# Streaming encoder step on one core: first tile's v-row sums moved into the u stage, the dots' x rows moved to SBUF, and the first tile's dots put ahead of later routing

## The chip, the core and the metric

The kernel runs on one core of one Trainium2 chip. The metric is the time of one execution on the device in microseconds (us), and lower is better. TensorE is PE in the rows, VectorE is DVE, ScalarE is ACT, GpSimd is POOL, SyncE is SP.

## What is computed

One layer for 1024 prompt tokens and 32 sample tokens of width 1024: sparse and forgetting attention, an output projection, cross-attention into 256 memory tokens, and a mixer that picks, for each token, 16 of 16384 single-neuron experts in each of 8 heads. The change is in the mixer:

```python
def blk(xb):                                  # 128 tokens
    q = (xb @ w_q).reshape(TOK_BLOCK, PEER_HEADS, PEER_KEY_DIM)
    s1 = jnp.einsum('thd,hnd->thn', q[..., :half], keys1)
    s2 = jnp.einsum('thd,hnd->thn', q[..., half:], keys2)
    v1, i1 = lax.top_k(s1, PEER_TOPK)
    v2, i2 = lax.top_k(s2, PEER_TOPK)
    ...
    g = jax.nn.softmax(sv, axis=-1)           # sv, eidx: the best 16 of the 16 x 16 sums
    h = jax.nn.gelu(jnp.einsum('td,thkd->thk', xb, u[eidx]), approximate=False)
    return jnp.einsum('thk,thkd->td', (g * h).astype(v.dtype), v[eidx])
```

## The kernel before

The 1056 tokens are split in two kinds. Four tiles of 128 tokens and the 32 sample tokens (544 tokens, columns 0 to NSP) are **sparse**: their chosen rows of u and v are gathered from HBM. Each gather is one indirect DMA that GpSimd issues; it takes its 128 row numbers from one column of an index tile in SBUF and brings 128 rows of 4 KB (0.52 MB), one per partition. One gather serves one token, whose 8 x 16 experts lie on the 128 partitions. The other 512 tokens are **dense**: they are multiplied with all experts.

The program is a row of blocks that follow each other on all engines. Those of interest:

- **Mixer stage** (dense tokens' projections, `route`, first part): 40 weight blocks of 128x1024 (8 w_out, 8 w_mq, then attention, 8 w_mo, 16 w_pq). Each is rounded by ScalarE, its remainder is taken by GpSimd ("split", L1041), and TensorE makes 24 matmuls of it (L1062).
- **u stage** (`route`, second part): 128 blocks of u. For each, ScalarE rounds (L1591), GpSimd splits (L1596, both inputs in SBUF), TensorE makes 24 matmuls (L1606), ScalarE applies Gelu (L1614), SyncE stores 256 KB and loads the block four further on (512 KB). There are two buffers: block n+2 is rounded when product n is done.
- **Gates stage** (`spread_gates`): one-hot matmuls for the dense tokens' gates, and 24 batches of v sums.
- **v stage** (`experts`): 128 blocks of v for the dense tokens (L2884, split on GpSimd at L2968), and between them the remaining v sums.

**Routing and dots.** VectorE does the top-k work in nine slots (`slot(j)`: tiles 0 to 3, the sample tokens, tiles 4 to 7), in 21 steps each. The list of routing instructions is a generator; `progress.fill(us)` in the mixer stage takes pieces up to a budget, and the u stage takes all the rest. Between the steps stand the **dots**: for token d, `dot(d)` (L1943) multiplies the gathered u row with the token's x row and sums to one column of `hn`. The x row of the current tile lies in PSUM (`row_flat`, 2 banks), spread over the partitions and put there by ScalarE in `show_rows`, which waits until the dots of the tile before are done. `DOTS_AT[j]` says how many dots go into slot j, `CHUNKS_AT[j]` how many u blocks TensorE does beside it.

**GpSimd's queue.** It holds split n+2 and then the gathers due beside block n, in that order, block after block. A gather waits until the dot that last used its row buffer is done (14 buffers in the u stage, 6 in the mixer stage). So gathers and splits share one queue in program order.

**v sums.** A batch is four tokens: four gathers of v rows, then 8 matmuls with the weights placed by ScalarE in a zero-padded tile (`SparseSum`, L2576). There are 136 batches, 24 in the gates stage (`B_STEPS`) and 112 in the v stage; TensorE takes them in its own queue between the products.

Of the kernel before, what the change touches and what calls it, by code (L numbers as in the profile page):

```python
# [14 lines left out]
P = 128  # L15
# [1522 lines left out]
PIECES = 40  # L1538
# [341 lines left out]
def route(nc, sem, dram, keep, mx, sems):  # L1880


    with ExitStack() as ctx:
# [6 lines left out]
        RINGS = (list(range(RING + 2)), list(range(RING + 10)))  # L1890
# [63 lines left out]
        def tail(j):  # L1954
# [33 lines left out]

        def slot(j):
# [4 lines left out]
            def ordered(op, cost):  # L1994
# [4 lines left out]
                yield cost  # L1999
                if j >= 1:  # L2000
                    yield from dots(DOTS_TO[j] + DOTS_AT[j] * min(done[0], 16) // 16)
# [184 lines left out]
        def beside_pieces(engine, u):  # L2186
# [7 lines left out]
            if u == len(LATE_UNITS) - 1:  # L2194
                reach(2, 0)

        late_attention(nc, sem, late_ctx, dram, keep, beside_load, beside_scores, beside_copy, beside_pieces)
        late_ctx.close()

        open_mixer(nc, ctx, keep, "n_", ND)  # L2200
        row_flat = keep["row_flat"]
# [3 lines left out]
                for part, a, n in (("ring", 0, RING), ("oS_flat", 2 * D, 2), ("oD_flat", 0, 4), ("q_flat", 0, 4))  # L2205
                for i in range(n)]
        hidden = DenseHidden(mx, keep, dram, mx.xh)
# [3 lines left out]
        ps, x_ps = keep["aps"][:, 0:2, :], keep["aps"][:, 2, 0:3 * P].rearrange("p (i m) -> p i m", i=3)  # L2211
        norm_q, norm_f = mx.norm(), mx.norm()
# [3 lines left out]
        def _(engine):  # L2216
# [11 lines left out]
            for n in range(MIX, QRY):  # L2228
                progress.fill(us)
                if n == QRY - 1:  # L2230
                    reach(2, TAIL)
# [6 lines left out]
            for n in range(QRY, ATT):  # L2238
                progress.fill(us)
                if n == QRY + 1:  # L2240
                    reach(2, TAIL + 1)
# [11 lines left out]
            for n in range(PKQ, END):  # L2253
                progress.fill(us + 1.0)
                if n == PKQ:
                    reach(3, S_DONE)
                if n == PKQ + 4:
                    reach(3, TAIL + 1)
# [7 lines left out]
        def _(sp):  # L2266
            load_pq(sp, 3)
            sp.wait_ge(mx.x_split, 28)
            sp.dma_start(mx.h, dram["xP"][:, :, mx.c0:mx.c0 + mx.w]).then_inc(h_loaded, 16)
            for n in range(2, 27):  # L2270
                mx.load(sp, n)
                if n == 15:
                    load_pq(sp, 4)
# [11 lines left out]
            for j in range(5, QT + 2):  # L2285
                if j < QT:
                    if j == 5:
# [3 lines left out]
                for n in chunks(j):  # L2291
                    hidden.store(sp, n)
                    if n + 4 < NKEY:
                        hidden.load(sp, n + 4)
            hidden.finish(sp)

        @block.tensor
        def _(pe):
# [30 lines left out]
            for n in range(QRY, ATT):  # L2329
# [4 lines left out]
                if n in (QRY + 1, QRY + 2):  # L2334
                    scores(3, n - QRY - 1)
                if n == QRY + 6:
                    turn(1)
# [7 lines left out]
            for n in range(PKQ, END):  # L2345
                mx.product(pe, n)
                if n in (PKQ + 3, PKQ + 4):
                    scores(4, n - PKQ - 3)
                if n == PKQ + 8:
                    turn(2)  # L2350
            for j in range(5, QT + 2):
# [14 lines left out]
        def _(act):  # L2366
# [11 lines left out]
            def show_rows(i):  # L2378

                if i > 0:  # L2380
                    act.wait_ge(x_loaded, 16 * i)
                    act.wait_ge(dotted, i * P)
                act.activation(row_flat, xrow[:, :], ACT.Copy).then_inc(row_shown, 1)
                if i < NS:
                    act.wait_ge(row_shown, i + 1)
                    act.dma_start(xrow[:, :], dram["s_x"][i]).then_inc(x_loaded, 16)

# [11 lines left out]
            show_rows(0)  # L2399
# [10 lines left out]
            for n in range(QRY, ATT):  # L2410
                next_high(n + 2)
                if n in (QRY + 2, QRY + 3):
                    copy_scores(3, n - QRY - 2)
                if n == QRY + 4:
                    exponents(act, 2)
                if n == QRY + 6:
                    keep_routes(act, 1)
# [837 lines left out]
```

## Time and profile before

| | us |
|---|---|
| median of 3 runs (3956.85 to 3971.69) | 3968.24 |
| profiled execution, its own time | 3969.84 |
| its span, first to last instruction | 3968.0 |
| mixer stage | 1357 to 1695 |
| u stage | 1695 to 2617 |
| gates stage | 2624 to 2850 |
| v stage | 2876 to 3940 |

The span of the profiled execution and its time differ by 1.8 us. PE is busy 88% of the span, DVE 62%, POOL 49%, ACT 29%. These are averages over stages with different limits, so they are to be read stage by stage: the digits of the page show POOL near idle in the first half and at 7 to 8 tenths in the u stage, where the DMA engines are at 9.

### The profile page before, as it was taken

The numbers are of one execution on the slowest core, as the hardware profiler recorded it, in microseconds if no ns is written. First come the engines' busy times: TensorE is split into PE (matmuls) and PEld (weight loads), VectorE is DVE, ScalarE is ACT, GpSimd is POOL, SyncE is SP. The second block draws the span as 40 slices with busy tenths as digits, with TensorE's granted clock in tenths as the row PEclk, the third lists the DMA queues.
The fourth block names the chain that finished last, engine by engine and source line by source line (L and its number), as shares of the span: only waits on it lengthen the run. The fifth ranks groups of instructions, "written<-read, shape, count | busy, mean of one in ns | idle before, by whom it ended". The sixth has DMA issues, their size and how long they took to land. (4 is left out here: it accounts for less than half of the span.)

```text
span 3968.0 us, 49765 instructions
## 1 busy us (share of the span) xinstructions
PE 3478.3 (88%) x17237; PEld 2501.8 (63%) x17237; DVE 2448.6 (62%) x5652; ACT 1158.6 (29%) x2264; POOL 1944.2 (49%) x1478
## 2 busy tenths in 40 slices
PE   7889887998989898887877878898689999999998
PEld 4445555788978676765666666665455556656655
DVE  3764423655857677779879697897633444434344
ACT  1213323121156523222222222266622212222222
POOL 0000001224400144778888888854267777877773
PEclk9888987998999999999999999999899999999999
DMA  2002103312431235799999999979998998989995
GB/s 117 10 33 61 55 27 123 101 54 87 140 96 33 85 121 191 278 348 377 399 396 401 400 396 401 374 253 400 329 366 324 363 360 336 392 339 351 358 374 217
DMA packets 335403, 978.48 MB, mean 247 GB/s; under 512 B 34400, under 2 KB 84456, under 8 KB 333648
## 3 DMA queue, kind: packets, MB, share of 16 engines
q0 software_dynamic: 156672, 570.49, 36.7%
q1 hardware_dynamic: 173584, 389.78, 27.9%
q10 hardware_dynamic: 4928, 15.34, 1.1%
q8 instruction: 130, 2.13, 0.2%
q14 instruction: 89, 0.73, 0.0%
HBM read 873.61 MB, written 101.89 MB: 246 GB/s over the span
## 5 line engine op out<-in xcount | busy, mean ns | idle before, releaser
L1606 PE MATMUL n_ps<-n_xh_flat,n_wh 128*128 128x512 f32 x3072 | 748.3, 401 | 162.8 <-POOL n_wh L1596 160.9
L2884 PE MATMUL e_y_ps<-e_wh,e_vh 128*128 128x512 f32 x3072 | 751.3, 401 | 45.4 <-DVE e_wh L3008 34.7
L1606 PEld LDWEIGHTS n_ps<-n_xh_flat,n_wh 128*128 128x128 f32 x3072 | 581.3, 192 | 325.2 <-POOL n_wh L1596 202.9
L2884 PEld LDWEIGHTS e_y_ps<-e_wh,e_vh 128*128 128x128 f32 x3072 | 572.1, 189 | 266.6 <-issue 130.4
L1025 POOL CAST m_wh<-raw 128x1024 fp32r<-128x1024 f32 x40 | 42.2, 1054 | 911.4 <-issue 659.0
L2968 POOL TENSOR_TENSOR e_vh<-raw,e_vh 128x1024 fp32r<-128x1024 f32 x128 | 309.2, 2418 | 225.9 <-ACT e_vh L2910 223.0
L3047 DVE TENSOR_TENSOR oT<-e_y_ps,oT 128x512 f32<-128x512 f32 x256 | 175.8, 691 | 376.0 <-PE e_y_ps L2884 303.6
L2543 POOL DMA_INDIRECT e_rows<-in_v,eid x346 | 349.1, 1009 | 99.0 <-issue 86.9
L1596 POOL TENSOR_TENSOR n_wh<-raw,n_wh 128x1024 fp32r<-128x1024 f32 x128 | 307.4, 2402 | 39.6 <-ACT n_wh L1591 37.3
L1943 DVE CUSTOM_DVE_ANT_0 oT<-oT,n_row_ps 128x1024 f32<-128x1024 f32 x227 | 270.9, 1217 | 67.9 <-DMA oT<-in_u,eid 64.4
L1062 PE MATMUL m_ps<-m_xh_flat,m_wh 128*128 128x272 f32 x1920 | 261.8, 298 | 40.7 <-DVE oT L1095 12.3
L1041 POOL TENSOR_TENSOR n_wh<-raw,n_wh 128x1024 fp32r<-128x1024 f32 x40 | 100.2, 2507 | 384.7 <-ACT n_wh L1035 384.3
L1062 PEld LDWEIGHTS m_ps<-m_xh_flat,m_wh 128*128 128x128 f32 x1920 | 254.7, 196 | 46.0 <-issue 20.6
L1062 PE MATMUL n_ps<-n_xh_flat,n_wh 128*128 128x512 f32 x960 | 240.7, 409 | 36.2 <-POOL n_wh L1041 14.9
L2576 PE MATMUL z_ps<-e_rows,flat 128*32 128x512 f32 x1384 | 255.2, 602 | 19.4 <-DMA e_rows<-in_v,eid 17.0
L1943 DVE CUSTOM_DVE_ANT_0 m_ring<-m_ring,n_row_ps 128x1024 f32<-128x1024 f32 x184 | 220.3, 1217 | 74.4 <-DMA m_ring<-in_u,eid 71.3
L1614 ACT ACTIVATE flat<-n_ps 128x512 f32<-128x512 f32 x128 | 76.5, 597 | 640.1 <-PE n_ps L1606 599.6
L2466 POOL DMA_INDIRECT oT<-in_u,eid x227 | 219.0, 965 | 62.2 <-issue 46.8
L1062 PEld LDWEIGHTS n_ps<-n_xh_flat,n_wh 128*128 128x128 f32 x960 | 185.2, 195 | 88.6 <-POOL n_wh L1041 28.2
L2910 ACT ACTIVATE e_vh<-raw 128x1024 fp32r<-128x1024 f32 x128 | 134.5, 1052 | 322.6 <-PE e_y_ps L2884 187.6
L2466 POOL DMA_INDIRECT m_ring<-in_u,eid x184 | 179.6, 976 | 69.8 <-issue 37.9
L1943 DVE CUSTOM_DVE_ANT_0 n_q_flat<-n_q_flat,n_row_ps 128x1024 f32<-128x1024 f32 x133 | 159.1, 1217 | 25.5 <-DMA n_q_flat<-in_u,eid 21.6
(390 smaller groups left out, 5698.1 us busy)
## 6 DMA issues: line engine op xcount, KB each, us to landing
raw<-in_ut SPq DMA_DIRECT2D x128, 512.0 KB
raw<-in_v SPq DMA_DIRECT2D x126, 512.0 KB
s_hid<-flat SPq DMA_DIRECT2D x128, 256.0 KB
xrow<-s_hid SPq DMA_DIRECT2D x126, 256.0 KB
s_gate<-g_stage SPq DMA_DIRECT2D x3, 8192.0 KB, 53.1
raw<-in_w_pq SPq DMA_DIRECT2D x32, 512.0 KB
m_ring<-s_gate SPq DMA_DIRECT2D x32, 512.0 KB
gh<-s_gate SPq DMA_DIRECT2D x32, 512.0 KB
```

The source lines that it names most:

```text
L1041: pool.tensor_tensor(wh[:, at % 2, LO, :], w[:, at % 2, :], wh[:, at % 2, HI, :].bitcast(F32), ALU.subtract).then_inc(self.w_split, 1)
L1062: mm = pe.matmul(self.bank(n, g), wh[:, at % 2, hw, k * P:(k + 1) * P], self.xh[:, hx, k, a:a + c], start=(k == 0 and o == 0), stop=(k == ...
L1596: pool.tensor_tensor(self.uh[:, at % 2, LO, :], self.u[:, at % 2], self.uh[:, at % 2, HI, :].bitcast(F32), ALU.subtract).then_inc(self.mx. ...
L1606: mm = pe.matmul(self.ps[:, n % 2, 0:ND], self.uh[:, at % 2, a, k * P:(k + 1) * P], self.xd[:, b, k, :], start=(k == 0 and o == 0), stop=( ...
L1943: dve.tensor_tensor_reduce(out=rows[b], in0=rows[b], in1=row_flat, scale=1.0, scalar=0.0, op0=ALU.mult, op1=ALU.add, accum_out=hn[:, d:d + ...
L2466: pool.indirect_dma_start(out=rows[b], out_offset=None, in_=dram["u"], in_offset=bass.IndirectOffsetOnAxis(ap=eid[:, d:d + 1], axis=0)).th ...
L2543: pool.indirect_dma_start(out=buffer, out_offset=None, in_=self.rows_dram, in_offset=bass.IndirectOffsetOnAxis(ap=self.idt[:, col:col + 1] ...
L2576: mm = pe.matmul(self.ps[g * 32:(g + 1) * 32, t % 2, half, :], self.wz[:, b // 4 % 2, b % 4 * P + g * 32:b % 4 * P + (g + 1) * 32], buffer ...
L2884: mm = pe.matmul(y_ps[:, o, 0:TD], vh[:, n % SLOT, a, m * P:(m + 1) * P], wh[n % SLOT][:, b, g * TD:(g + 1) * TD], start=(c == 0 and e == ...
L2910: act.activation(vh[:, n % SLOT, HI, :], v[:, n % 2, :], ACT.Copy).then_inc(v_rounded, 1)
L2968: pool.tensor_tensor(vh[:, n % SLOT, LO, :], v[:, n % 2, :], vh[:, n % SLOT, HI, :].bitcast(F32), ALU.subtract).then_inc(v_split, 1)
L3047: dve.tensor_tensor(y[:, m, cols], y_ps[:, o % 4, 0:TD], y[:, m, cols], ALU.add).then_inc(y_added, 1)
```

## The change

1. The **32 batches of the first tile** (v sums of tokens 0 to 127) are summed in the u stage, between blocks 22 and 122, in two PSUM banks of their own (`y_ps`), with their gathers in GpSimd's queue. The result goes to HBM (`s_ysp`) and is loaded again in the v stage, where it is turned and added as before. The gates stage still sums 24 batches (those of tile 1), the v stage 80 instead of 112.
2. The **x rows** of the dots lie in SBUF (`xrow` and a new `x_row`, loaded by DMA from `s_x`), no more in PSUM; `show_rows` falls away. The dot's three tensors are then all in SBUF.
3. The **128 dots of tile 0** stand in the last steps of routing slot 2, ahead of the routing of slots 3 to 8. Slots 3 and 4 keep their order, but slot 4's u blocks are now beside slot 3's routing (`FIRST_IN_U` 4), and the blocks per slot are redistributed. The row buffers are 10 instead of 14 in the u stage (the other four hold v rows and weights).
4. ScalarE's Gelu and the weighting of tile 0 come at block 12, the turn at block 18. GpSimd begins with 14 semaphore clears.

```diff
-CHUNKS_AT = (0, 0, 0, 0, 0, 18, 32, 32, 30, 12, 4)
+FIRST_IN_U = 4
+CHUNKS_AT = (0, 0, 0, 0, 27, 22, 22, 22, 21, 10, 4)
-DOTS_AT = (0, 0, 0, 64, 64, 128, 128, 128, 32, 0)
+DOTS_AT = (0, 0, 128, 64, 64, 64, 64, 80, 80, 0)
+WEIGH_AT, GELU_BLOCK, TURN_BLOCK, SUM_FROM, SUM_TO = (3, 8), 12, 18, 22, 122
+SUM_BLOCKS = tuple(SUM_FROM + b * (SUM_TO - SUM_FROM) // 31 for b in range(32))
...
-            dve.wait_ge(row_shown, d // P + 1)
+            i = d // P
+            if i > 0:
+                dve.wait_ge(x_loaded[i % 2], 16 * ((i + 1) // 2))
             b = ring.take(now[0])
             dve.wait_ge(row_ready[b], 16 * ring.uses(d))
-            dve.tensor_tensor_reduce(out=rows[b], in0=rows[b], in1=row_flat,
+            dve.tensor_tensor_reduce(out=rows[b], in0=rows[b], in1=x_rows[i % 2],
...
+        sums.ps = ctx.enter_context(nc.psum_tensor("y_ps", [P, 1, 2, 512], F32))
-        row_flat = keep["row_flat"]
+        x_rows = [xrow[:, :], sb("x_row", [P, D])[:, :]]
...
@@ tensor, u stage
                     hidden.product(pe, n)
+                    if n == TURN_BLOCK:
+                        pe.wait_ge(weighed, 1)
+                        pe.matmul(w_ps, hn[:, 0:P], ident, start=True, stop=True).then_inc(weights_turned, 1)
+                    for b in range(32):
+                        if SUM_BLOCKS[b] == n:
+                            at = [(4 * b + g) % N_ROW for g in range(4)]
+                            sums.sum(pe, b, [v_rows[i] for i in at], [v_row_ready[i] for i in at],
+                                     [16 * ((4 * b + g) // N_ROW + 1) for g in range(4)])
@@ gpsimd, u stage
-                    last = min(DOTS_TO[j] + 10, N_DOT)
+                    last = max(first, min(DOTS_TO[j] + 7, N_DOT))
                     gathers(first + -(-(last - first) * (i + 1) // CHUNKS_AT[j]))
+                    while batch < 32 and GELU_BLOCK < n and SUM_BLOCKS[batch] <= n + 6:
+                        for g in range(4):
+                            i_row = 4 * batch + g
+                            if i_row >= N_ROW:
+                                pool.wait_ge(sums.summed, (i_row - N_ROW) // 4 + 1)
+                            sums.gather(pool, batch, g, v_rows[i_row % N_ROW], v_row_ready[i_row % N_ROW])
+                        batch += 1
@@ v stage
+B_FIRST = 32
+            act.dma_start(ysp[:, :], dram["s_ysp"]).then_inc(ysp_loaded, 16)
```

GpSimd's queue in the middle of the u stage, before. `n_wh` is the split of a u block, `in_u,eid` a gather of u rows for a dot, and x is a count:

```order
301 L1596 TENSOR_TENSOR n_wh<-raw,n_wh 128x1024
302 L2466 DMA n_q_flat<-in_u,eid 128x1024 x3
303 L2466 DMA m_ring<-in_u,eid 128x1024
304 L1596 TENSOR_TENSOR n_wh<-raw,n_wh 128x1024
305 L2466 DMA m_ring<-in_u,eid 128x1024 x3
306 L2466 DMA oT<-in_u,eid 128x1024
307 L1596 TENSOR_TENSOR n_wh<-raw,n_wh 128x1024
```

The same queue in the changed kernel, where `in_v,r_idt` are the gathers of a batch's four v rows:

```order
326 L1598 TENSOR_TENSOR n_wh<-raw,n_wh 128x1024
327 L2505 DMA oT<-in_u,eid 128x1024 x3
328 L1598 TENSOR_TENSOR n_wh<-raw,n_wh 128x1024
329 L2505 DMA m_ring<-in_u,eid 128x1024 x3
330 L2591 DMA n_q_flat<-in_v,r_idt 128x1024 x4
331 L1598 TENSOR_TENSOR n_wh<-raw,n_wh 128x1024
```

Three u gathers a block stand here instead of four, and behind every third or fourth block come four v gathers. Over the whole queue there are 71 u gathers ahead of the u stage and 473 in it before, and 128 ahead and 416 with 128 v gathers in it now.

VectorE's dots in the u stage, before and now. The second input is the x row, `n_row_ps` in PSUM before and `r_x_row` (or `xrow`) in SBUF now:

```order
1851 L1943 ISA n_q_flat,gh<-n_q_flat,n_row_ps 128x1024
1852 L1943 ISA gh 128x1
1853 L1943 ISA n_q_flat,gh<-n_q_flat,n_row_ps 128x1024
1854 L1943 ISA gh 128x1
1855 L1943 ISA n_q_flat,gh<-n_q_flat,n_row_ps 128x1024
```

```order
2555 L1949 ISA oT,gh<-oT,r_x_row 128x1024
2556 L1949 ISA gh 128x1
2557 L1949 ISA oT,gh<-oT,r_x_row 128x1024
2558 L1949 ISA gh 128x1
2559 L1949 ISA oT,gh<-oT,r_x_row 128x1024
```

Count and shape of the dots are as they were; their second input has moved from PSUM to SBUF.

TensorE in the u stage now has the sums of a batch (`y_ps`, 8 matmuls) between the products (24 matmuls for each u block), where before there were products and routing scores alone:

```order
635 L1608 MATMUL n_ps<-n_xh_flat,n_wh 128x512 x96
636 L2625 MATMUL y_ps<-n_q_flat 32x512 x8
637 L1608 MATMUL n_ps<-n_xh_flat,n_wh 128x512 x72
638 L2625 MATMUL y_ps<-m_mk_p,n_q_flat 32x512 x2
639 L2625 MATMUL y_ps<-m_mv_p,n_q_flat 32x512 x2
```

In the v stage the batches (`z_ps`) stood behind every 24 matmuls and are now behind 48 and 24 in turn.

## Rows read from the trace of the kernel before

**Rows 1.** Stages: us; busy PE, PEld, DVE, ACT, POOL; clock, DMA share, GB/s.

```profile
1357.00:1695.00 338.00, 293.38 (x1289) 232.73 (x1289) 247.45 (x652) 100.89 (x160) 179.96 (x116) 0.94 0.58 200
1695.00:2617.00 922.00, 760.91 (x3212) 597.53 (x3213) 784.46 (x2006) 227.12 (x294) 755.52 (x600) 0.98 1.00 384
2876.00:3940.00 1064.00, 1023.19 (x4903) 637.48 (x4902) 449.54 (x529) 227.79 (x323) 753.94 (x574) 0.99 0.91 348
```

**Rows 2.** One cycle of the u stage, in order of time, starts and durations in us.

```profile
1999.56 5.73 PE L1606 MATMUL n_ps<-n_xh_flat,n_wh 128*128 128x512 f32 x24 [1.51 <-POOL n_wh L1596]
2003.42 0.94 POOL L2466 DMA_INDIRECT oT<-in_u,eid  x1 [0.30 <-DVE gh L1943]
2004.38 2.37 POOL L1596 TENSOR_TENSOR n_wh<-raw,n_wh 128x1024 fp32r<-128x1024 f32 x1
2006.80 5.78 PE L1606 MATMUL n_ps<-n_xh_flat,n_wh 128*128 128x512 f32 x24 [1.50 <-POOL n_wh L1596]
...
2007.10 1.22 DVE L1943 CUSTOM_DVE_ANT_0 m_ring<-m_ring,n_row_ps 128x1024 f32<-128x1024 f32 x1 [2.53 <-DMA m_ring<-in_u,eid]
```

**Rows 3.** Waits in the u stage: us in total, times, longest.

```profile
PE n_ps L1606 <- POOL n_wh L1596: 160.9, 93, 5.8
...
POOL n_wh L1596 <- ACT n_wh L1591: 35.4, 19, 6.9
...
ACT n_row_ps L2383 <- DVE gh L1943: 23.5, 3, 8.9
```

**Rows 4.** VectorE instructions with two SBUF inputs beside GpSimd's, in order of time.

```profile
1413.09 2.29 DVE L2088 TENSOR_TENSOR oT<-con,r_sab 128x2048 f32<-128x2048 f32 x1
1413.16 4.49 POOL L1041 TENSOR_TENSOR n_wh<-raw,n_wh 128x1024 fp32r<-128x1024 f32 x1 [3.91 <-ACT n_wh L1035]
...
1655.66 2.29 DVE L2088 TENSOR_TENSOR oT<-con,r_sab 128x2048 f32<-128x2048 f32 x1
1655.95 2.81 POOL L2466 DMA_INDIRECT oT<-in_u,eid  x1 [0.30 <-issue]
...
3307.95 2.40 POOL L2968 TENSOR_TENSOR e_vh<-raw,e_vh 128x1024 fp32r<-128x1024 f32 x1 [2.25 <-ACT e_vh L2910]
3308.43 2.47 DVE L3008 TENSOR_TENSOR e_wh<-xrow,e_wh 128x512 fp32r<-128x512 f32 x1 [0.59 <-ACT e_wh L2918]
```

**Rows 5.** Groups of the u stage: count, busy us, mean ns, idle before.

```profile
L2466 POOL DMA_INDIRECT n_q_flat<-in_u,eid x133 | 125.2, 941 | 35.4 <-issue 29.3 <-DVE gh L1943 5.5
L1943 DVE CUSTOM_DVE_ANT_0 n_q_flat<-n_q_flat,n_row_ps 128x1024 f32<-128x1024 f32 x133 | 159.1, 1217 | 25.5 <-DMA n_q_flat<-in_u,eid 21.6 <-issue 2.9
```

**Rows 6.** Groups of the v stage.

```profile
L2543 POOL DMA_INDIRECT e_rows<-in_v,eid x346 | 349.1, 1009 | 99.0 <-issue 86.9 <-PE z_ps L2576 9.6
L3008 DVE TENSOR_TENSOR e_wh<-xrow,e_wh 128x512 fp32r<-128x512 f32 x127 | 140.3, 1116 | 29.1 <-ACT e_wh L2918 25.2
L2884 PE MATMUL e_y_ps<-e_wh,e_vh 128*128 128x512 f32 x3072 | 751.3, 401 | 45.4 <-DVE e_wh L3008 34.7 <-issue 10.7
```

**Rows 7.** Durations of one v-stage VectorE line, ns min/median/max.

```profile
L3008 DVE TENSOR_TENSOR e_wh<-xrow,e_wh x128: 677/692/3169, 2874.7 to 3894.3; 128x512 fp32r<-128x512 f32 x128
```

**Rows 8.** TensorE in the v stage: one batch between two products.

```profile
3311.48 5.85 PE L2884 MATMUL e_y_ps<-e_wh,e_vh 128*128 128x512 f32 x24
3317.26 1.92 PE L2576 MATMUL z_ps<-e_rows,flat 128*32 128x512 f32 x16
```

**Rows 9.** Products of the mixer stage: w_mo's first, w_pq's first, u's first.

```profile
1524.23 16.62 PE L1062 MATMUL n_ps<-n_xh_flat,n_wh 128*128 128x512 f32 x72 [1.41 <-DVE n_xh_flat L1234]
...
1566.40 6.02 PE L1062 MATMUL n_ps<-n_xh_flat,n_wh 128*128 128x512 f32 x24
1584.62 5.64 PE L1062 MATMUL n_ps<-n_xh_flat,n_wh 128*128 128x512 f32 x12 [9.36 <-DVE n_xh_flat L1118]
...
1695.04 16.93 PE L1606 MATMUL n_ps<-n_xh_flat,n_wh 128*128 128x512 f32 x72 [1.78 <-ACT flat L1129]
```

**Rows 10.** GpSimd's waits in the mixer stage.

```profile
POOL n_wh L1041 <- ACT n_wh L1035: 102.8, 23, 20.1
```

More of the change, by code:

```diff
@@ L1987, in keep_ids, with weigh_first @@
             n_eid[0] += 1
+        def weigh_first():
+            dve.wait_ge(kept, 1)
+            dve.scalar_tensor_tensor(out=idt0[:, :], in0=routes[:, 0, 0:P], scalar=float(NKEY), in1=routes[:, 1, 0:P],
+                                     op0=ALU.mult, op1=ALU.add).then_inc(idt_ready, 1)
+            dve.memset(sums.zero[:, :, :], 0.0).then_inc(sums.cleared, 1)
+            dve.wait_ge(gelued, 1)
+            dve.wait_ge(gn_ready, 1)
+            dve.tensor_tensor(hn[:, 0:P], hn[:, 0:P], gn[:, 0:P], ALU.mult).then_inc(weighed, 1)
         def slot(j):
@@ L2284, in _ @@
                 hidden.load(sp, n)
-            for j in range(5, QT + 2):
+            shown = 1
+            for j in range(FIRST_IN_U, QT + 2):
                 if j < QT:
-                    if j == 5:
+                    if j == FIRST_IN_U:
                         for b in range(2):
@@ L2451, in _ @@
         def _(pool):
+            for past in late_sems:
+                pool.sem_clear(past)
             done = [0]
@@ L2492, in _ @@
                 hidden.split(pool, n)
-            for j in range(5, QT + 2):
+            batch = 0
+            for j in range(FIRST_IN_U, QT + 2):
                 first = done[0]
@@ L2504 @@
 LAST_OF = tuple(32 * t + 31 for t in range(NS)) + (N_BATCH - 1,)
-TURNS = tuple(33 * t + 34 for t in range(NS)) + (N_BATCH + NS,)
-N_STEP = N_BATCH + NS + 1
+B_FIRST = 32
 B_STEPS = 24
+TURNS = (B_STEPS + 1,) + tuple(33 * t + 2 for t in range(1, NS)) + (N_BATCH - B_FIRST + NS,)
+N_STEP = N_BATCH - B_FIRST + NS + 1
 def batch_at(s):
-    return s - sum(s > t for t in TURNS)
+    return B_FIRST + s - sum(s > t for t in TURNS)
 def tile_of_batch(b):
@@ L2604, in spread_gates @@
         gelued, weighed, turned, idt_ready = (sem("g_" + n) for n in ("gelued", "weighed", "turned", "idt_ready"))
-        row_ready = [sem(f"g_row{b}_ready") for b in range(N_ROW)]
+        row_ready, rows_before = keep["v_row_ready"], 4 * B_FIRST // N_ROW
         NB, NQ = ND // TB, TB // 4
@@ L2635, in turn_weights @@
                 pe.wait_ge(weighed, 1)
-                for t in range(NS):
-                    pe.matmul(sums.ps[:, 1, 0, t * P:(t + 1) * P], hn[:, t * P:(t + 1) * P], ident,
+                for t in range(1, NS):
+                    pe.matmul(sums.ps[:, 0, 0, t * P:(t + 1) * P], hn[:, t * P:(t + 1) * P], ident,
                               start=True, stop=True)
@@ L2658, in _ @@
                         at = [(4 * b + g) % N_ROW for g in range(4)]
-                        sums.sum(pe, b, [rows[:, i, :] for i in at], [row_ready[i] for i in at],
-                                 [16 * ((4 * b + g) // N_ROW + 1) for g in range(4)])
+                        sums.sum(pe, B_FIRST + b, [rows[:, i, :] for i in at], [row_ready[i] for i in at],
+                                 [16 * (rows_before + (4 * b + g) // N_ROW + 1) for g in range(4)])
         @block.gpsimd
```

206 lines of the change are left out of this document (113 added, 93 removed).

## The prediction

> **What bounds the kernel now.** I read the stages first. In the u stage the DMA share is 1.00 at 384 GB/s, PE is busy 761 of 922 us and POOL 756 [rows 1], so none is plainly idle, and the question is which one sets the pace. The timeline of one cycle shows it. A product begins at 1999.56 and the next at 2006.80, 7.24 us apart, though 24 matmuls need only 5.8; PE waits 1.5 us for the split. POOL in turn goes straight from its last gather (3.42 to 4.36) into the split [rows 2]: its queue holds four gathers of 0.95 and 0.30 between them and a split of 2.37, 4 x 1.25 + 2.4 = 7.4 us. Over the stage PE waits 160.9 us for POOL's splits, while POOL waits only 35.4 for ScalarE [rows 3]. So **GpSimd's queue sets the u stage**, with the DMA engines as full as it. A check by the whole stage: 112 blocks with 451 gathers are 112 x 2.4 + 451 x 1.25 = 833 us, and the last 16 blocks, whose 22 gathers fit under the products, are 16 x 5.85 = 94. The sum of 927 meets the measured 922.
>
> The v stage is TensorE's: busy 1023 of 1064 us [rows 1], with a batch of sums between two products taking 1.92 us [rows 8] and the products 751.3 [rows 6].
>
> The mixer stage has slack on POOL (180 busy of 338 [rows 1], 102.8 waited for ScalarE [rows 10]), and its pace is that of the products, 6.0 us a block in w_mo and (1695.04 - 1584.62) / 16 = 6.9 in w_pq [rows 9].
>
> **A lock between VectorE and GpSimd.** This is the row on which most rests. A VectorE instruction with two SBUF inputs (L2088) runs 1413.09 to 1415.38. The split that begins at 1413.16 takes 4.49 us instead of 2.40: it did nothing until VectorE was through. A **gather** that begins at 1655.95, under the same kind of instruction, takes 2.81 instead of 0.94 and ends 0.81 after it. The other way round, L3008 of 128x512 begins at 3308.43 inside a split and takes 2.47 [rows 4] where its median is 0.692 [rows 7]. The dots of before have one input in PSUM and show nothing of it: 1217 ns in mean, and gathers beside them 941 [rows 5].
>
> The Trainium skill (SBUF - State Buffer, Who interferes with whom) says that a VectorE instruction with two SBUF inputs contends with a GpSimd instruction that reads SBUF, and not with one that only writes; the splits agree (4.49 us). It also infers that descriptor generation, needing the write side, isn't held by a tensor_tensor. If gathers were free of it, only the 168 splits would pay. Here the row speaks against that, since the gather of 2.81 us was held.
>
> **The change part by part**, against the profiled execution (3969.8 us, 1.6 above the median shown).
>
> *v stage, 32 batches fewer.* Each is 1.92 us of PE with its rows at hand [rows 8]: 61 us. Waits for rows go with some of them: (1064 - 751 - 35 of waiting for `e_wh` [rows 1, 6]) / 112 = 2.5 us a batch, turns, norms and all waits included, is the most that one costs. Between the two I take 2.35, **-75**, from -61 to -105 (80, and 25 if a gather load a quarter lighter also removes waits of the other 80 batches).
>
> *GpSimd's queue in the u stage.* 71 more gathers (416 + 128 for 473). By the same sum: 124 blocks with 544 gathers are 124 x 2.4 + 544 x 1.25 = 978, and 4 blocks by PE 23, together 1001. Against 927: **+74** (up to 89, if the former last blocks were not PE's). The products and sums of PE, 748 + 32 x 1.9 = 809, stay below. The bytes say the same: 922 us x 384 GB/s = 354 MB, plus 71 x 0.524 = 37, is 391 MB, 980 to 1018 us at 399 to 384 GB/s. Neither resource offers a way around the other.
>
> *The lock in the u stage.* 416 dots of 1.22 us now have two SBUF inputs, and no row shows this instruction in that form. Below, the price is nothing (if it takes its x row another way); above, each GpSimd instruction could meet a dot just begun. Nearest is the v stage. There L3008's 127 instructions [rows 6] of 0.69 [rows 7] and as many of L3003, also with two SBUF inputs, fill 175 of 1064 us, 0.165; a GpSimd instruction that falls in one waits half of it, 0.165 x 0.345 = 0.057 us in mean. The gathers there take 1009 ns in mean, 0.070 over 939 [rows 6], so chance overlap gives it, and a little more. For the dots: 416 x 1.22 = 508 us of some 1170 is 0.43; times half of 1.22 is 0.26 us, or 0.30 with the same surplus. I take 0.28 for each of 544 gathers and 128 splits: 672 x 0.28 = **+188**, on the queue that sets the stage. Bounds: 0.10 (dots run mostly while rows are missing and POOL is past its read), +67; 0.50 (dot and gather, both some 1.25 us long, fall into step so that each gather meets the next dot), +336.
>
> *VectorE in the u stage.* It is held by splits too, up to 128 x 2.4 = 307 us. Its work: 784 us now [rows 1] less 473 dots of 1.30 (1.22 [rows 5] and the readout) = 169 of routing for 4.9 slots, 34.5 a slot. After: 6 x 34.5 + 416 x 1.30 = 748, with all stalls 1055, under the 1184 that the queue takes. So it isn't the bound, only close to it.
>
> *The mixer stage.* 128 gathers instead of 71. By the order, 96 of them come beside the 24 blocks of w_mo and w_pq and the attention between, some 78 beside the blocks, 3.25 each: 2.4 + 3.25 x 1.25 + 4.25 x 0.28 = 7.7 us on POOL, against (8 x 6.0 + 16 x 6.9) / 24 = 6.6. That is 1.1 x 24 = 26, and VectorE, whose `add_out` stands behind dots that a split holds for up to 2.4 us, adds in w_mq and w_mo perhaps 14: **+40**. From +12 (its slack takes it) to +80 (VectorE held in 40 blocks by 2 us).
>
> *`show_rows` gone.* ScalarE waited there 23.5 us in three places [rows 3] with Gelu and rounding behind it. POOL was busy with its gathers in most of it: **-10**, from 0 to -24.
>
> *At nothing:* the gates stage has the same 24 batches; the shorter Gelu and multiply are off its loop. Store and load of `s_ysp` (0.5 MB) lie beside products. The 14 clears come where POOL waits for the first rounding. At block 12 POOL's next split stands behind the wait for `idt0`, made by VectorE after dot 160, whose row is gathered in block 11; up to 10 us once, inside the range. ScalarE's `place` waits on sums made two blocks before. PE's turn at block 18 waits on work finished by 14.
>
> Sum: 3969.8 - 75 + 74 + 188 + 40 - 10 = 4187. I predict **4185 us**, 5.5% slower.
>
> **The rivals.**
>
> 1. *Only splits are held, not gathers.* For it speaks the page's inference; against it the 2.81 us row. 128 x 0.28 = 36 in place of 188 and 25 in the mixer: 3970 - 75 + 74 + 36 + 25 - 10 = 4020. Chance 0.12.
> 2. *No hold at all* (the dot is a custom instruction, and no row shows it with two SBUF inputs): 3970 - 75 + 74 + 12 - 10 = 3971, no change. Chance 0.07.
> 3. *Faster.* One mechanism: the v stage's PE loses its row waits too (-105), and that outweighs the u stage's queue. With the queue at +74, +5 in the mixer and -24: 3920. It decides only from a lock price below 30 us in both stages, against [rows 4]. Chance 0.08.
> 4. *Dots and gathers in step, or VectorE the bound.* A gather read falls each 1.24 us, a dot each 1.14 to 1.30; at 0.50 us a piece the u stage takes 336 more and the mixer 80: about 4375. Chance 0.10.
>
> **How the numbers follow.** My forecast (4080 to 4340) has 0.63. With rival 1 (4000 to 4080) that is 0.75, so the range takes in the half of rival 4 that lies below 4380 too: 4000 to 4380 leaves out 0.20, rivals 2 and 3 and the rest of 4. The lower bounds of the lock's price (4066 - 28 in the mixer) lie inside. About 0.5% (20 us) is what a measurement of this kernel tells from no change. Faster 0.08, within 0.08 (rival 2 and a sliver of the neighbours), slower 0.84.
>
> **What would show it.** In the profile after: gathers in the u stage at 1.15 to 1.3 us in mean instead of 0.95, with a tail to 2.1; splits at 2.6 to 2.8; dots that begin in a split at up to 3.5 us, and a dot mean near 1.8; the u stage at 1130 to 1230 us with a DMA share under 0.9; the v stage at 960 to 1000 us with PE still over 95%; w_pq blocks at 7.5 to 8.5 us. A gather mean under 1.0 would prove the lock term wrong; a v stage over 1010 us the gain; a DVE busy nearly all of the u stage would mean that it, not POOL, is the bound.

## The result, and the profile after

The changed kernel takes **4142.4 us** (median of 4 runs, 4135.5 to 4146.6) where the kernel before takes 3968.1 on the same chip: ratio 1.0443, interval 1.0417 to 1.0468. The profiled execution of it took 4146.6 us, its span is 4144.8.

The stages of the changed kernel, in the columns of [rows 1]: mixer, u and v stage.

```profile
1358.00:1755.00 397.00, 306.68 (x1255) 239.30 (x1255) 280.88 (x485) 95.38 (x151) 284.85 (x173) 0.89 0.73 243
1755.00:2946.00 1191.00, 896.11 (x3764) 669.46 (x3764) 875.60 (x2177) 234.05 (x319) 1006.39 (x673) 0.87 0.93 330
...
3201.00:4115.00 914.00, 894.86 (x4387) 616.09 (x4388) 489.99 (x526) 225.92 (x305) 633.78 (x446) 0.99 0.88 333
```

Against [rows 1] the mixer stage is 59 us longer, the u stage 269 longer, the v stage 150 shorter, and the gates stage as before (260 us from the last product of u to the first of v, before 258). The sum is +178, and the medians say +174. The DMA share of the u stage fell from 1.00 to 0.93 although more rows are moved there, and GpSimd rose from 756 of 922 us to 1006 of 1191. So the queue of GpSimd still sets the pace; it has 71 gathers more, and its entries have become longer. The groups of the u stage on GpSimd (count, busy us, mean ns, idle before), to be held against [rows 5]:

```profile
L2505 POOL DMA_INDIRECT oT<-in_u,eid x248 | 322.3, 1299 | 69.7 <-issue 60.9 <-DVE gh L1949 5.8
L1598 POOL TENSOR_TENSOR n_wh<-raw,n_wh 128x1024 fp32r<-128x1024 f32 x127 | 315.2, 2482 | 16.7 <-ACT n_wh L1593 14.7
L2505 POOL DMA_INDIRECT m_ring<-in_u,eid x168 | 214.2, 1275 | 43.6 <-issue 42.4
L2591 POOL DMA_INDIRECT n_q_flat<-in_v,r_idt x64 | 79.5, 1243 | 19.5 <-issue 19.5
L2591 POOL DMA_INDIRECT m_mk_p<-in_v,r_idt x32 | 37.7, 1178 | 9.8 <-issue 9.8
L2591 POOL DMA_INDIRECT m_mv_p<-in_v,r_idt x32 | 36.7, 1148 | 9.8 <-issue 9.5 <-PE y_ps L2625 0.3
```

A gather takes 690.4 / 544 = 1.27 us in mean instead of 0.94 to 0.96. GpSimd waits for ScalarE 14.7 us only, and TensorE for GpSimd's splits 292.8 us (before 160.9, [rows 3]):

```profile
PE n_ps L1608 <- POOL n_wh L1598: 292.8, 69, 12.4
```

What makes a gather long is to be seen in the timeline of the changed kernel (start, duration):

```profile
2202.60 0.27 DVE L2057 MAX8 r_v<-oT 128x8 f32<-128x128 f32 x1
2202.61 0.94 POOL L2591 DMA_INDIRECT m_mv_p<-in_v,r_idt  x1 [0.30 <-issue]
...
2203.57 2.36 POOL L1598 TENSOR_TENSOR n_wh<-raw,n_wh 128x1024 fp32r<-128x1024 f32 x1
...
2204.86 2.15 DVE L1949 CUSTOM_DVE_ANT_0 oT<-oT,xrow 128x1024 f32<-128x1024 f32 x1
...
2206.08 1.76 POOL L2505 DMA_INDIRECT oT<-in_u,eid  x1 [0.16 <-issue]
...
2206.95 1.22 DVE L1949 CUSTOM_DVE_ANT_0 oT<-oT,xrow 128x1024 f32<-128x1024 f32 x1
...
2208.09 1.21 DVE L1949 CUSTOM_DVE_ANT_0 oT<-oT,xrow 128x1024 f32<-128x1024 f32 x1
2208.15 1.97 POOL L2505 DMA_INDIRECT oT<-in_u,eid  x1 [0.30 <-issue]
```

Beside VectorE's top-k work, the gather at 2202.61 takes 0.94. The dot at 2204.86 begins inside a split that ends at 2205.93 and takes 2.15, until 1.08 after the split. The gather at 2206.08 begins inside this dot, which ends at 2207.01, and ends 0.83 after it; the next dot, begun at 2206.95, no longer holds it. The gather at 2208.15 falls just behind the start of a dot and takes 1.97. So each waits out what the other has begun, as in [rows 4].

Counted over the whole u stage from the timeline, 260 of the 544 gathers begin inside a dot. They take 1.55 us in mean, and 251 of them end 0.8 us after that dot; the other 284 take 1.01. Experiment 2 below, with the x row in PSUM, has as many inside a dot (272), and those take 0.94. A few are held much longer: six take over 2.4 us. The longest begins 0.12 us behind the start of a dot, three further dots follow back to back, and it ends 0.83 us after the last of them, which ends at 1973.45:

```profile
1968.82 1.20 DVE L1949 CUSTOM_DVE_ANT_0 oT<-oT,r_x_row 128x1024 f32<-128x1024 f32 x1
1968.94 5.34 POOL L2505 DMA_INDIRECT oT<-in_u,eid  x1 [0.16 <-issue]
...
1972.24 1.21 DVE L1949 CUSTOM_DVE_ANT_0 oT<-oT,r_x_row 128x1024 f32<-128x1024 f32 x1
```

In the v stage the rows of v are never late (groups of TensorE's sums there, with no idle time before them):

```profile
L2625 PE MATMUL z_ps<-e_rows,flat 128*32 128x512 f32 x992 | 153.0, 598 | 0.0
L2625 PE MATMUL z_ps<-m_ring,flat 128*32 128x512 f32 x288 | 68.8, 598 | 0.0
```

### The profile page after: what moved, and what is told of

Same layout as the page of the kernel before. It is cut to its first block and busy times, and to the rows that moved or that the text cites. A ratio compares the mean times of both kernels' runs of the same rounds, so it can differ in the third digit from the quotient of the medians.

```text
span 4144.8 us, 49656 instructions
## 1 busy us (share of the span) xinstructions
PE 3497.9 (84%) x17237; PEld 2558.4 (62%) x17237; DVE 2610.6 (63%) x5655; ACT 1157.2 (28%) x2262; POOL 2182.2 (53%) x1480
## 5 line engine op out<-in xcount | busy, mean ns | idle before, releaser
L1608 PE MATMUL n_ps<-n_xh_flat,n_wh 128*128 128x512 f32 x3072 | 819.4, 429 | 293.0 <-POOL n_wh L1598 292.8
L1608 PEld LDWEIGHTS n_ps<-n_xh_flat,n_wh 128*128 128x128 f32 x3072 | 635.7, 210 | 483.3 <-POOL n_wh L1598 328.3
L2505 POOL DMA_INDIRECT oT<-in_u,eid x290 | 380.0, 1310 | 87.4 <-issue 70.5
L2505 POOL DMA_INDIRECT m_ring<-in_u,eid x254 | 334.8, 1318 | 80.8 <-issue 63.1
L1598 POOL TENSOR_TENSOR n_wh<-raw,n_wh 128x1024 fp32r<-128x1024 f32 x128 | 317.5, 2481 | 16.8 <-ACT n_wh L1593 14.7
L1062 PE MATMUL n_ps<-n_xh_flat,n_wh 128*128 128x512 f32 x960 | 253.8, 425 | 72.1 <-POOL n_wh L1041 50.5
L1949 DVE CUSTOM_DVE_ANT_0 m_ring<-m_ring,xrow 128x1024 f32<-128x1024 f32 x150 | 225.3, 1529 | 110.8 <-DMA m_ring<-in_u,eid 110.3
L2591 POOL DMA_INDIRECT e_rows<-in_v,eid x248 | 253.7, 1023 | 75.2 <-issue 61.6
L1949 DVE CUSTOM_DVE_ANT_0 oT<-oT,r_x_row 128x1024 f32<-128x1024 f32 x152 | 208.8, 1401 | 120.9 <-DMA oT<-in_u,eid 120.4
L1062 PEld LDWEIGHTS n_ps<-n_xh_flat,n_wh 128*128 128x128 f32 x960 | 194.1, 205 | 132.0 <-POOL n_wh L1041 69.9
L1041 POOL TENSOR_TENSOR n_wh<-raw,n_wh 128x1024 fp32r<-128x1024 f32 x40 | 99.1, 2479 | 330.4 <-ACT n_wh L1035 329.9
L1949 DVE CUSTOM_DVE_ANT_0 oT<-oT,xrow 128x1024 f32<-128x1024 f32 x138 | 198.0, 1457 | 78.3 <-DMA oT<-in_u,eid 77.6
L1949 DVE CUSTOM_DVE_ANT_0 m_ring<-m_ring,r_x_row 128x1024 f32<-128x1024 f32 x104 | 153.8, 1499 | 76.6 <-DMA m_ring<-in_u,eid 75.7
```

The source lines that it names most:

```text
L1041: pool.tensor_tensor(wh[:, at % 2, LO, :], w[:, at % 2, :], wh[:, at % 2, HI, :].bitcast(F32), ALU.subtract).then_inc(self.w_split, 1)
L1062: mm = pe.matmul(self.bank(n, g), wh[:, at % 2, hw, k * P:(k + 1) * P], self.xh[:, hx, k, a:a + c], start=(k == 0 and o == 0), stop=(k == ...
L1598: pool.tensor_tensor(self.uh[:, at % 2, LO, :], self.u[:, at % 2], self.uh[:, at % 2, HI, :].bitcast(F32), ALU.subtract).then_inc(self.mx. ...
L1608: mm = pe.matmul(self.ps[:, n % 2, 0:ND], self.uh[:, at % 2, a, k * P:(k + 1) * P], self.xd[:, b, k, :], start=(k == 0 and o == 0), stop=( ...
L1949: dve.tensor_tensor_reduce(out=rows[b], in0=rows[b], in1=x_rows[i % 2], scale=1.0, scalar=0.0, op0=ALU.mult, op1=ALU.add, accum_out=hn[:, ...
L2505: pool.indirect_dma_start(out=rows[b], out_offset=None, in_=dram["u"], in_offset=bass.IndirectOffsetOnAxis(ap=eid[:, d:d + 1], axis=0)).th ...
```

## The experiments

The stops of TensorE for batches in the v stage are measured below in one way: the time from the end of one product to the start of the next where sums of v rows and nothing else stand between, added up over the stage from the timeline. Before: 108 such stops, 283 us. Changed kernel: 76 stops, 136 us, 1.78 each. A stop with its rows at hand is 1.78 in both, so some 90 of the 283 us (283 - 108 x 1.78) were lost to late rows, in 37 stops of more than 2.3 us.

**1. The lock alone.** In the kernel before, the x row goes to SBUF:

```diff
-        row_flat = keep["row_flat"]
+        row_flat = sb("x_row", [P, D])[:, :]
```

> The kernel before with one change: the x row that all 544 dots read lies in an SBUF tile instead of PSUM (ScalarE still copies it there, order and gathers are as before). Theory of the lock (a dot with two SBUF inputs holds the index read of a gather and the reads of a split): 473 gathers of the u stage cost about 0.33 us more each and its 128 splits 0.08, so the u stage goes from 922 to some 1090 us (1060 to 1130), the mixer stage gains 5 to 20 us, and the time is 4145 us (4110 to 4175); gathers of u rows in the u stage at 1.2 to 1.35 us in mean. Rival (the order of the dots and the v gathers made the changed kernel slow, not the place of the x row): no change, 3968 us, gathers at 0.94.

Measured: 4182.7 us, ratio 1.0545 (1.0511 to 1.0579). This one edit costs 214 us; the 4182.7 are 8 above the top of what I expected. Windows of its mixer and u stage, and GpSimd's groups in the latter:

```profile
1357.00:1706.00 349.00, 296.62 (x1290) 234.99 (x1291) 268.21 (x652) 101.01 (x160) 204.02 (x116) 0.93 0.58 194
1706.00:2821.00 1115.00, 849.16 (x3215) 658.06 (x3215) 924.45 (x1994) 225.97 (x295) 963.43 (x600) 0.89 0.92 318
```

```profile
L1596 POOL TENSOR_TENSOR n_wh<-raw,n_wh 128x1024 fp32r<-128x1024 f32 x127 | 309.3, 2435 | 18.4 <-ACT n_wh L1591 16.2
L2466 POOL DMA_INDIRECT oT<-in_u,eid x204 | 279.6, 1371 | 54.8 <-issue 53.0 <-DVE gh L1943 0.9
L2466 POOL DMA_INDIRECT m_ring<-in_u,eid x136 | 196.1, 1442 | 36.3 <-issue 35.1
L2466 POOL DMA_INDIRECT n_q_flat<-in_u,eid x133 | 179.1, 1347 | 38.6 <-issue 34.0 <-DVE gh L1943 3.5
```

The u stage is 193 us longer, the mixer stage 11, and 16 more lie between the last product of u and the first of v (274 us, before 258), whose cause is open. A gather takes 654.9 / 473 = 1.38 us, the splits (2435 ns) hardly more than before. The rival is out: the old order is slowed as well. And the hold is nearly all on the gathers, not on the splits.

**2. The changed kernel without the lock.** The x row is back in PSUM, the early sums stay. To make room, the sums take the banks of the scores, and these are made in quarters:

```diff
-CHUNKS_AT = (0, 0, 0, 0, 27, 22, 22, 22, 21, 10, 4)
-DOTS_AT = (0, 0, 128, 64, 64, 64, 64, 80, 80, 0)
+CHUNKS_AT = (0, 0, 0, 0, 25, 20, 20, 20, 29, 10, 4)
+DOTS_AT = (0, 0, 128, 64, 64, 64, 64, 128, 32, 0)
...
-            dve.tensor_tensor_reduce(out=rows[b], in0=rows[b], in1=x_rows[i % 2],
+            dve.tensor_tensor_reduce(out=rows[b], in0=rows[b], in1=row_flat,
...
-        sums.ps = ctx.enter_context(nc.psum_tensor("y_ps", [P, 1, 2, 512], F32))
+        sums.ps = keep["aps"][:, 0:2, :].unsqueeze(1)
+        row_flat = ctx.enter_context(nc.psum_tensor("n_row_ps", [P, 2, 512], F32))[:, :, :].rearrange("p a b -> p (a b)")
```

> The changed kernel with the x row back in PSUM. The 32 early batches stay in the u stage; their sums lie in two banks that the routing scores used there, and those scores are made in quarters in another bank; the dots of the last tile stand in slot 7 and the blocks per slot are shifted to fit. Theory of the lock: the mean of a gather in the u stage falls from 1.27 to 0.95 us, the u stage from 1191 to about 1000 us (the queue sum of before with 71 more gathers, 995), the v stage stays at 914, the mixer stage falls to 350 to 385, and the time is 3925 us (3890 to 3965), under that of before. Rival (the additional v gathers and the new order cost more than the queue sum says): u stage over 1060 us, time over 4000.

Measured: 3948.6 us, ratio 0.9956 (0.9939 to 0.9974), just under the kernel before. Its mixer, u and v stage:

```profile
1357.00:1706.00 349.00, 289.93 (x1254) 228.30 (x1252) 247.88 (x484) 95.20 (x150) 229.53 (x173) 0.93 0.77 275
1706.00:2740.00 1034.00, 859.74 (x3764) 646.07 (x3764) 801.80 (x2175) 239.80 (x324) 846.60 (x673) 0.91 0.99 380
...
2998.00:3911.00 913.00, 894.50 (x4384) 616.17 (x4385) 472.32 (x525) 226.78 (x304) 632.14 (x446) 0.99 0.89 333
```

Gathers in its u stage take 539.1 / 544 = 0.99 us. This is the largest group of them:

```profile
L2506 POOL DMA_INDIRECT oT<-in_u,eid x248 | 248.0, 1000 | 70.8 <-issue 50.1 <-DVE gh L1947 20.0
```

The u stage is 1034 us where the queue sum says 995; its DMA share is 0.99, and 1034 x 380 GB/s = 393 MB is what the bytes asked for. The DMA engines, not only the queue, are full. That gathers take 0.99 us and not 0.95 has another reason: 19 of the 544 take more than 1.1 us (4 of 473 in the kernel before), 17 of them under top-k instructions with two SBUF inputs, and all others take 0.94 in mean. One of them, and a split under the next such instruction:

```profile
2046.37 2.28 DVE L2108 TENSOR_TENSOR oT<-con,r_sab 32x2048 f32<-32x2048 f32 x1
2046.53 2.94 POOL L2506 DMA_INDIRECT oT<-in_u,eid  x1 [0.30 <-issue]
2048.68 2.28 DVE L2113 TENSOR_TENSOR oT<-oT,r_fi 32x2048 f32<-32x2048 f32 x1
2049.49 3.69 POOL L1598 TENSOR_TENSOR n_wh<-raw,n_wh 128x1024 fp32r<-128x1024 f32 x1
```

**3. The lock put back into it.** Its counter-test:

```diff
-        row_flat = ctx.enter_context(nc.psum_tensor("n_row_ps", [P, 2, 512], F32))[:, :, :].rearrange("p a b -> p (a b)")
+        row_flat = sb("x_row", [P, D])[:, :]
```

> The previous kernel (changed kernel without two-SBUF-input dots, early sums kept) with the one edit that puts the x row in an SBUF tile again. Theory of the lock: the u stage is 170 to 200 us longer than with the x row in PSUM, gathers at 1.27 us in mean, time 4120 us (4090 to 4160), close to the changed kernel. Rival (the redistribution of dots and scores, not the lock, made the difference): within 20 us of the previous kernel.

Measured: 4149.2 us, ratio 1.0468 (1.0431 to 1.0505), 200.6 above the kernel without the lock and near the changed one. Its mixer and u stage:

```profile
1356.00:1751.00 395.00, 303.41 (x1255) 237.00 (x1256) 285.46 (x485) 96.06 (x151) 279.14 (x173) 0.90 0.73 245
1751.00:2936.00 1185.00, 885.19 (x3764) 661.61 (x3762) 900.29 (x2172) 237.15 (x323) 1013.37 (x673) 0.87 0.94 331
```

So the lock costs 151 us in the u stage (1185 - 1034) and 46 in the mixer stage (395 - 349). The other differences between this kernel and the changed one (redistributed dots, scores in quarters, `show_rows`) come to 7 us, 4149.2 against 4142.4, so next to nothing.

**4. The v stage: fewer batches.** The v stage had shrunk by 150 us where I had said 75. Four kernels leave out parts of 32 of the 112 batches of the kernel before, spread evenly. The first leaves out both parts:

```diff
+OUT_OF = tuple(b for b in range(B_STEPS, 136) if b % 4 == 1 or b in (50, 74, 98, 122))
...
             def gather(b):
 
+                if b in OUT_OF:
+                    return
...
-        for half in range(2):
+        for half in range(1 if few else 2):
             for g in range(4):
                 if half == 0:
                     pe.wait_ge(ready[g], counts[g])
+                if few and g < 3:
+                    continue
```

> The kernel before, with 32 of the 112 batches of the v stage left out as far as possible: their 128 gathers are not made, and of their 8 matmuls one is left (it sums a quarter of the rows of the batch before), so the sums of those tokens are missing. They are spread evenly. The changed kernel's v stage was 150 us shorter where I had said 75. Theory that both is the work itself (fewer batches, and the other 80 cheaper because rows come sooner): v stage 1064 to 920 us (905 to 945), time 3825. Rival (only 75 come from the batches, the rest from where the changed kernel's remaining batches stand or from its other edits): v stage 980 to 1000, time about 3895.

Measured: 3893.2 us, ratio 0.9812 (0.978 to 0.9845): the rival's figure. But the stops still held some 40 us of late rows, and the reason was the experiment's own: a batch left out counted as one of the two that GpSimd gathers ahead. Three further kernels split it up. The first of them leaves out seven of the eight matmuls and keeps all gathers:

> The kernel before; all gathers stay, but of 32 of the 112 batches of the v stage, spread evenly, TensorE makes one matmul instead of eight, so these tokens' sums are incomplete. It separates TensorE's work from the late rows: in the v stage of before 67 of 110 stops for a batch take under 1.9 us and 28 take over 3, because rows come late, 88 us in all. Theory (late rows come from GpSimd's queue, a split and four gathers in 7.5 us for each slot of TensorE's 7.7): with TensorE's slots shorter and the queue as full as before, the rows are later still, and of 32 x 1.4 = 45 us of TensorE's work less than half is gained: time 3945 to 3970. Rival (each part pays for itself): 3923.

Measured: 3951.4 us, ratio 0.9952 (0.9932 to 0.9972). The next leaves out the gathers and keeps all matmuls, and GpSimd is again two batches with gathers ahead:

```diff
-                    goal = min(batch_at(steps_before(p, i)) + 2, N_BATCH)
+                    goal, n_kept = batch_at(steps_before(p, i)), 0
+                    while goal < N_BATCH and n_kept < 2:
+                        n_kept += goal not in OUT_OF
+                        goal += 1
```

> The kernel before; all matmuls stay, but the 128 gathers of 32 of the 112 batches of the v stage are left out (these batches sum the rows of the batch before once more, so these tokens' sums are wrong), and GpSimd gathers two real batches ahead as in the original. Theory (late rows are the missing half of the v stage's gain): nearly all 88 us of late rows vanish with TensorE's work unchanged, v stage 1064 to 985 us, time 3885 (3875 to 3905). Rival (the gain sits in TensorE's work and where the batches stand): under 20 us, 3950 or more.

Measured: 3893.9 us, ratio 0.981 (0.9787 to 0.9833). The last leaves out both, with the same lead:

> As the earlier kernel that leaves out gathers and seven of eight matmuls of 32 batches, but GpSimd again gathers two real batches ahead (there it was sometimes one, because a left-out batch counted as one of the two; 17 batches still stopped for rows, 52 us in all). Theory (late rows explain the rest): v stage 1064 to 930 us, time 3835 (3825 to 3850), close to what the changed kernel's v stage gains. Rival (where the changed kernel's batches stand, or another of its edits): 3893 again.

Measured: 3861.7 us, ratio 0.9737 (0.9716 to 0.9759), 12 above the range expected, and 32 below the 3893 of the rival.

Leaving out matmuls alone gains 14 us, gathers alone 72, both 104. The stops for batches add up to 260, 206 and 176 us (before 283). With the gathers alone gone, TensorE makes all its sums and loses 206 - 192 = 14 us to late rows. With the matmuls gone and the gathers kept, the saved time is mostly waited away: its stops with one matmul take 2.2 us in mean, where those of the last kernel take 0.93. That last one fell short of 3835 because that single matmul costs more than I had counted: 32 x (1.78 - 0.93) = 27 us of matmuls were left out, not 45, and some 10 us of late rows stayed.

**5. More lead, nothing left out.** The kernel before, complete, with one number changed:

```diff
-                    goal = min(batch_at(steps_before(p, i)) + 2, N_BATCH)
+                    goal = min(batch_at(steps_before(p, i)) + 3, N_BATCH)
```

> The kernel before, complete, with one number changed: in the v stage GpSimd gathers three batches ahead instead of two (the 13 row buffers hold 3.25 batches). Theory (a row is late because its gather is issued only in the slot before its use, behind a split that waits for ScalarE): with a slot more of lead the bursts are smoothed and 40 to 80 of the 88 us of late rows vanish, time 3890 to 3930. Rival (GpSimd's queue is simply too long for the slots, lead or not): at most 10 us, 3958 to 3975.

Measured: 3899.8 us, ratio 0.9821 (0.9796 to 0.9847). One place shows why. In the kernel before (timeline of the v stage) a batch starts at 3071.52 and lasts to 3080.2, because its four rows come one by one:

```profile
3071.52 1.02 PE L2576 MATMUL z_ps<-e_rows,flat 128*32 128x512 f32 x2 [0.99 <-issue]
3072.72 1.04 PE L2576 MATMUL z_ps<-e_rows,flat 128*32 128x512 f32 x2 [0.17 <-DMA e_rows<-in_v,eid]
3074.80 1.04 PE L2576 MATMUL z_ps<-e_rows,flat 128*32 128x512 f32 x2 [1.04 <-DMA e_rows<-in_v,eid]
3076.98 3.21 PE L2576 MATMUL z_ps<-e_rows,flat 128*32 128x512 f32 x10 [1.13 <-DMA e_rows<-in_v,eid]
```

The four gathers of these rows begin at 3061.26 to 3065.27, 6 to 10 us ahead of the batch, where those of the batch before began 12 to 15 us ahead of theirs. GpSimd had got to work late: its split had waited for ScalarE with these gathers behind it, and ScalarE, which clears and places the weights of later batches, had itself waited for sums of TensorE.

```profile
3057.17 0.23 ACT L2557 ACTIVATE flat<-flat 128x16 f32<-128x16 f32 x1 [13.05 <-PE z_ps L2576]
...
3058.69 2.41 POOL L2968 TENSOR_TENSOR e_vh<-raw,e_vh 128x1024 fp32r<-128x1024 f32 x1 [6.54 <-ACT e_vh L2910]
```

With a batch more of lead the gathers of this batch begin at 3054.22 to 3058.07, the same place is a batch of 1.92 us, and no sum of the stage waits for a row:

```profile
3070.86 1.92 PE L2576 MATMUL z_ps<-e_rows,flat 128*32 128x512 f32 x16
```

```profile
L2576 PE MATMUL z_ps<-e_rows,flat 128*32 128x512 f32 x1384 | 214.4, 598 | 0.0
L2576 PE MATMUL z_ps<-m_ring,flat 128*32 128x512 f32 x408 | 99.1, 598 | 0.0
```

The stops fall to 203 us (the 11 above 108 x 1.78 are waits of the products behind them for VectorE, not of sums for rows), from the first product of v to the last it is 993 us instead of 1062, and the gather load is that of before. The rival (the queue is too long) is out: it was how early the gathers stand in the queue, not how many there are.

**6. The order alone, and the two gains together.** The kernel before with the first tile's dots early (`FIRST_IN_U`, `CHUNKS_AT` and `DOTS_AT` as in experiment 2), all x rows in PSUM, all sums where they were; then the same with the lead of three.

> The kernel before with only the new order of dots and routing: the 128 dots of the first tile ahead of the routing of slots 3 to 8, slot 4's blocks beside slot 3, all x rows in PSUM, all sums in the gates and v stages as before. 57 gathers move from the u stage to the mixer stage. Theory (the order itself is a gain, the u stage costs 1.25 us of GpSimd's queue for each gather): u stage 922 to 845 us (416 gathers: 124 x 2.4 + 416 x 1.25 + 23 = 841), mixer stage +12 as in the kernel without the lock, time 3900 us (3885 to 3925). Rival (the first tile's early dots cost the mixer stage and VectorE what they save): 3955 to 3985.

Measured: 3936.2 us, ratio 0.9936 (0.991 to 0.9962), 11 us above the range I had given.

> The previous kernel and, in the v stage, gathers three batches ahead instead of two. Theory (the two are independent: one shortens GpSimd's queue in the u stage, the other takes away late rows in the v stage, 66 us): 3835 us (3815 to 3860). Rival (what the u stage gains comes back later): 3870 or more.

Measured: 3867.4 us, ratio 0.9763 (0.9738 to 0.9788), the fastest complete kernel of all, but 7 us above the range I had given and only 3 below the figure of the rival. It is the order that fell short, not the sum of the two: the second gain is fully there (3936.2 - 3867.4 = 69), the first is a third of what I said (23 us, from 3959.6 on the same chip, for 68). The u stage of the first of them:

```profile
1707.00:2577.00 870.00, 766.83 (x3250) 605.35 (x3250) 782.22 (x2169) 236.49 (x307) 710.01 (x543) 0.97 0.99 374
```

It takes 870 us for the 841 of the queue sum. GpSimd is busy 710 of it, 111 are the usual gaps of up to 0.3 us between its entries, which the sum counts, and beyond those it waits 34 us for ScalarE and 6 for dots. The sum leaves such waits out outside the last blocks; that is where its 29 us are missing. A further 10 us lie behind the stage, 268 us from the last product of u to the first of v where it was 258, so a part of what the u stage gains does come back later; why was not tried.

## Why the prediction was right, and where its terms were off

The forecast of 4185 us (4000 to 4380) is 43 above the 4142 measured, and its mechanism is shown by experiments 1 and 3: a dot with two SBUF inputs holds GpSimd's gathers. Term by term:

- **Lock in the u stage, +188.** 151 (experiment 3 against 2). The price of a gather was right: 694.9 us for the 544 against 539.1 is 0.29 apiece, where I took 0.28. So was its make-up: I said that 0.43 of them meet a dot and wait half of 1.22 us, and 260 of 544, 0.48, begin in one and take 1.55 - 0.94 = 0.61 longer. The splits were wrong: 2504 ns with the lock and 2420 without is 0.08 us, not 0.28. I had put the same price on both kinds, as if a split fell on a dot by chance. But it stands right behind a gather, which ends some 0.8 us after a dot, and back-to-back dots begin every 1.14 us: of the 56 splits of the changed kernel that begin in a dot, half find 0.44 us of it or less left. Gathers and splits together are 156 + 11 = 167 us; 15 of it came back, since GpSimd waits less for ScalarE when its own entries are longer (10.7 us instead of 24.6).
- **GpSimd's queue, +74.** 112 without the dots' lock (experiment 2): 1034 us, against 922. Nearly all of it is in the gathers: with the gaps before them the 473 took 577 us and the 544 take 687, 87 for the 71 more at 1.22 and 23 because they are 0.04 dearer each, which is the lock again, of the top-k instructions. My sum took 15 us off, since it let the 22 gathers of the last 16 blocks before cost nothing; the upper bound of 89 that I gave, without that, was nearer.
- **Mixer stage, +40.** 59, of which 11 is there without the lock (experiment 2: new order and early gathers) and 48 with it (46 in experiment 3); w_pq blocks were said to take 7.5 to 8.5 us and took (1755 - 1615) / 16 = 8.7.
- **v stage, -75.** -150; this is the step that failed. I priced a batch at 2.35 us, between 1.92 and 2.5, as if each of the 112 were a little dear. In truth most cost 1.8 and 37 up to 9.6. That comes to 32 x 1.78 = 57 us of work and some 90 of late rows, and *all* of those vanished, also for the other 80 batches. My bound allowed 25 us for that. Experiments 4 and 5 show the late rows as the larger part: without a quarter of the gathers 14 us of them are left, and with all gathers but more lead none.
- **`show_rows`, -10.** Not tried by itself, and no gain is to be seen: the kernel of experiment 3, which keeps it, has a u stage of 1185 us, the changed kernel 1191.

The terms as measured (u stage 112 + 151 and 6 not separated, mixer stage 59, v stage -150) give the 178 between the two profiles. Forecast less measured is +75 for the v stage and +37 for the lock, -38 for the queue, -19 for the mixer stage, -10 for `show_rows`: 45, and 39 without the 6 that are not separated. So the total came nearer than its largest term because some errors had opposite signs. That part is luck; the direction is not, since the lock alone costs 201 to 214 us.

The rivals: *only splits are held* (4020) is refuted by gathers of 1.27 and 1.38 us. The Trainium skill (SBUF - State Buffer, Who interferes with whom) infers that a tensor_tensor does not stall descriptor generation. For an indirect gather the rows show the opposite: 2.81 us [rows 4] and 2.94 (experiment 2) beside a tensor_tensor with two SBUF inputs, and in experiments 1 and 3 0.43 and 0.29 us in mean by the dots. What the Trainium skill states there of a GpSimd instruction that reads SBUF fits these gathers, which take their row numbers from a tile in SBUF; whether the read of the numbers is what is held was not tried apart. *No hold at all* (3971) is refuted by the same rows. *Faster* (3920) had the v stage at -105, nearer than the forecast though still too small, and experiment 2 is what the change comes to with the lock away (3949, 0.4% faster). *In step, or VectorE the bound* did not come: gathers stayed at 1.27, and VectorE was busy 876 of 1191 us.

Of the signs that I named, the gather mean (1.27 us) and the length of the u stage (1191) were right. Splits at 2.48 us were said to take 2.6 to 2.8, the DMA share of 0.93 to be under 0.9, and the v stage of 914 us to be 960 to 1000. The dot mean was wrong too: I said near 1.8 us, and the groups of dots in the changed kernel's u stage have means of 1401 to 1506 ns:

```profile
L1949 DVE CUSTOM_DVE_ANT_0 oT<-oT,r_x_row 128x1024 f32<-128x1024 f32 x152 | 208.8, 1401 | 120.9 <-DMA oT<-in_u,eid 120.4
...
L1949 DVE CUSTOM_DVE_ANT_0 oT<-oT,xrow 128x1024 f32<-128x1024 f32 x98 | 145.3, 1506 | 57.5 <-DMA oT<-in_u,eid 57.0
```

Most dots meet no split: the median is 1.2 us, 59 of 419 take over 1.5, and the longest takes 4.3.

## What to carry to other kernels

A move that frees PSUM by giving a VectorE instruction a second SBUF input was paid for here on GpSimd's queue, by its gathers above all; look whether that queue sets the pace of the stage before making it. A mean per item hides two populations: when a few items carry the waits (here 37 of 108 stops), taking load away can remove all the waits at once, and so can a little more lead in the queue that issues the loads, which here gave 66 us for one number. Where an in-order queue holds both loads and work that waits for another engine, as GpSimd's did here, look whether its lead covers that wait.

## What was not expected of the hardware

- The hold nearly always ends with the dot that runs when the gather begins (251 of 260 gathers): the one at 2206.08 ended 0.83 us after that dot although the next dot had begun at once. A few are held longer: the one at 1968.94 was held through four dots in a row, to 0.83 us after the last. What decides between the two is open.
- TensorE's granted clock in the u stage fell with its waits: 0.98 before, 0.91 without the lock, 0.87 in the changed kernel, and a matmul of the products took 401, 416 and 429 ns. These are means between the two levels, 2.4 and 1.2 GHz, of which the lower had a larger share where TensorE waited more. Its price was not tried apart; TensorE waited 173 and 293 us for splits in the same stages of the latter two, so little of it can have shown.
- A batch cut to one 32-column matmul stops TensorE between two products for 0.93 us in mean, a whole one of eight (sixteen records) for 1.78 (experiment 4).
